# Turning the attention probabilities by a product with a diagonal tile of gate over sum

## The reference, cut to what matters

```python
pc = masked_softmax(lc, ...)          # compressed: 31 key blocks
ps = masked_softmax(ls, ...)          # selected: with 512 tokens all 8 blocks are taken, so plain causal attention
pw = masked_softmax(lw, ...)          # window of 512: causal attention again, other keys and values
o = gt[..., 0:1] * oc + gt[..., 1:2] * osel + gt[..., 2:3] * ow
```

## Time and profile before

| | us |
|---|---|
| runs, median (lowest to highest) | 2557.04 (2553.45 to 2559.98) |
| the profiled execution, its own time | 2555.5 |
| its span in the profile | 2553.8 |
| TensorE matmul busy | 2346.4 (92% of the span) |
| VectorE / ScalarE / GpSimd busy | 1055.2 / 582.3 / 1050.9 |
| mean granted TensorE clock | 0.959 of full speed |

### The profile page before, as it was taken

How to read it: one execution, slowest core, us unless ns; L and a number is a source line. 1 busy time by engine, 2 the same in 40 slices (tenths; PEclk the granted TensorE clock), 3 DMA queues, 4 the chain that set the end, 5 groups by cost and what they waited for, 6 DMA issues and landing times. The chain is left out here.

```text
span 2553.8 us, 38390 instructions
## 1 busy us (share of the span) xinstructions
PE 2346.4 (92%) x15304; PEld 1761.1 (69%) x15304; DVE 1055.2 (41%) x1959; ACT 582.3 (23%) x1339; POOL 1050.9 (41%) x920
## 2 busy tenths in 40 slices
PE   6999899789999999999996999999998999999998
PEld 4776444446777777666774768777775767777776
DVE  2001677354440232267887535354444034312421
ACT  1001566331000000135553423242331010000001
POOL 1331344245654464365653122121115546544643
PEclk9999799899999999999998999999999999999998
DMA  6632100361112211321116020020202122112211
GB/s 243 216 101 90 33 1 1 133 216 65 71 50 99 83 66 54 116 76 66 66 67 58 6 78 25 21 84 14 92 6 103 66 83 83 61 72 83 83 66 38
DMA packets 49947, 193.74 MB, mean 76 GB/s; under 512 B 15650, under 2 KB 24610, under 8 KB 33522
## 3 DMA queue, kind: packets, MB, share of 16 engines
q1 hardware_dynamic: 45490, 174.88, 20.3%
q0 software_dynamic: 3856, 15.61, 1.9%
q10 hardware_dynamic: 432, 0.88, 0.1%
HBM read 170.80 MB, written 28.81 MB: 78 GB/s over the span
## 5 line engine op out<-in xcount | busy, mean ns | idle before, releaser
L1631 PE MATMUL ps<-hid,ring 128*128 128x288 f32 x768 | 194.8, 410 | 23.0 <-DVE hid L1738 23.0
L1631 PE MATMUL ps<-xn,ring 128*128 128x288 f32 x768 | 202.7, 413 | 8.3 <-DVE xn L1722 7.8
L1631 PEld LDWEIGHTS ps<-hid,ring 128*128 128x128 f32 x768 | 146.4, 191 | 64.8 <-DVE hid L1738 24.9
L1631 PEld LDWEIGHTS ps<-xn,ring 128*128 128x128 f32 x768 | 146.6, 192 | 53.5 <-issue 8.0
L1659 ACT ACTIVATE p<-ps 128x288 f32<-128x288 f32 x48 | 19.7, 410 | 626.0 <-PE ps L1631 626.0
L218 PE MATMUL ps<-xn,ring 128*128 128x288 f32 x640 | 157.2, 409 | 3.8 <-ACTq L562 3.8
L1704 POOL TENSOR_TENSOR prod<-prod,rstd 128x1152 f32<-128x1152 f32 x32 | 83.8, 2620 | 179.7 <-DVE prod L1784 163.3
L218 PEld LDWEIGHTS ps<-xn,ring 128*128 128x128 f32 x640 | 122.6, 192 | 38.0 <-ACTq L562 3.9
L2868 PE MATMUL ps<-xn,ring 128*128 128x288 f32 x512 | 138.3, 416 | 3.6 <-PE ps L2933 3.6
L744 POOL TENSOR_SCALAR ring<-ring,fac 128x128 f32<-128x128 f32 (+2 forms) x96 | 92.2, 976 | 108.2 <-DVE fac L976 108.2
L1631 PE MATMUL ps<-x_sum,wsum 128*128 128x288 f32 x512 | 133.7, 415 | 3.2 <-DVE x_sum L1725 2.5
(11 more groups left out here) (471 smaller groups left out, 4838.1 us busy)
## 6 DMA issues: line engine op xcount, KB each, us to landing
ring<-in_w_mlp SPq DMA_DIRECT2D x64, 1024.0 KB, 4.9
ring<-in_w_gdn_in SPq DMA_DIRECT2D x16, 1024.0 KB, 4.9
ring<-in_w_nsa_in SPq DMA_DIRECT2D x10, 1024.0 KB, 8.5
ring<-in_w_gdn_z SPq DMA_DIRECT2D x8, 1024.0 KB, 4.9
x<-in_seq_state SPq DMA_DIRECT2D x4, 2048.0 KB, 8.3
out_seq_state<-x SPq DMA_DIRECT2D x4, 2048.0 KB, 11.1
ring<-in_w_gdn_out SPq DMA_DIRECT2D x8, 1024.0 KB, 5.7
out_win_old<-in_win_rows POOLq DMA_DIRECT2D x1, 8064.0 KB, 47.3
```

Of the source, the lines that this page charges most:

```text
L1631: mm = nc.tensor.matmul(S.ps[:, base + BANK[p], 0:HT], stationary(p, blk.units[pair // 4], pair % 4), moving(blk.kind, p, pair), start=pai ...
```

## The change

The probabilities are no longer scaled. GpSimd instead builds for each job and half, from the identity and `fac`, four diagonal tiles of 128 by 128 in one instruction (`diag`, two buffers), and `turn` multiplies each block of unscaled exponentials by the diagonal tile of its query tile i: the block is the stationary operand as before, the diagonal tile the moving one. The result is the block turned and each query column scaled by fac. The six GpSimd scalings and the two VectorE scalings of a job go; a transpose becomes a float32 product. `diag_set` takes the place of `scaled` and `last_scaled`, and GpSimd waits for the last turning of two jobs back before it writes `diag`. The whole diff:

```diff
--- before.py
+++ after.py
@@ -666,6 +666,7 @@
         rsum = sb("rsum", [128, 2, 2, PT])
         rcp = sb("rcp", [128, 2, PT])
         fac = sb("fac", [128, 2, 2, PT])
+        diag = sb("diag", [128, 2, 2, PT, 128])
         cneg = sb("cneg", [128, PT * NC])
         csc = sb("csc", [128, PT, 2, 40])
         cprob = sb("cprob", [128, PT, 2, NC])
@@ -674,8 +675,7 @@
         sem = S.sem
         vt_mm, vt_out, consts, neg_set = sem("pa_vt_mm"), sem("pa_vt_out"), sem("pa_consts"), sem("pa_neg_set")
         score, biased, maxed, exped = sem("pa_score"), sem("pa_biased"), sem("pa_maxed"), sem("pa_exped")
-        fac_step, fac_set, scaled = sem("pa_fac_step"), sem("pa_fac_set"), sem("pa_scaled")
-        last_scaled = sem("pa_last_scaled")
+        fac_step, fac_set, diag_set = sem("pa_fac_step"), sem("pa_fac_set"), sem("pa_diag_set")
         turned, turned_out, pv = sem("pa_turned"), sem("pa_turned_out"), sem("pa_pv")
         cmp_read, cstep, cexp, cready = sem("pa_cmp_read"), sem("pa_cstep"), sem("pa_cexp"), sem("pa_cready")
         cpv, o_done, o_out = sem("pa_cpv"), sem("pa_o_done"), sem("pa_o_out")
@@ -738,10 +738,12 @@
             nc.gpsimd.memset(csc[:], 0.0).then_inc(consts, 1)
             for job in range(NJ):
                 pool.wait_ge(fac_set, job + 1)
+                if job >= 2:
+                    pool.wait_ge(turned, chunk_no[job - 2, 1, 2] + 1)
                 for half in range(2):
-                    for i in range(PT - 1):
-                        p = prob[job % 3][half][:, p_at(i):p_at(i) + width(i)]
-                        nc.gpsimd.tensor_scalar(p, p, fac[:, job % 2, half, i:i + 1], None, ALU.mult).then_inc(scaled, 1)
+                    nc.gpsimd.tensor_tensor(diag[:, job % 2, half], S.c("ident").unsqueeze(1).broadcast_to([128, PT, 128]),
+                                            fac[:, job % 2, half].unsqueeze(2).broadcast_to([128, PT, 128]), ALU.mult
+                                            ).then_inc(diag_set, 1)
 
         @block.tensor
         def _(pe):
@@ -785,13 +787,13 @@
             def turn(job, g):
                 for half in range(2):
                     n = chunk_no[job, half, g]
-                    pe.wait_ge(scaled, (job * 2 + half + 1) * (PT - 1))
-                    pe.wait_ge(last_scaled, job * 2 + half + 1)
+                    pe.wait_ge(diag_set, job * 2 + half + 1)
                     if n >= 2:
                         pe.wait_ge(turned_out, n - 1)
                     for x, (j, i) in enumerate(blocks_of(g)):
-                        mm = nc.tensor.transpose(S.ps[:, TB + n % 2, 128 * x:128 * x + 128],
-                                                 prob[job % 3][half][:, p_at(i) + 128 * j:][:, 0:128], S.c("ident"))
+                        mm = nc.tensor.matmul(S.ps[:, TB + n % 2, 128 * x:128 * x + 128],
+                                              prob[job % 3][half][:, p_at(i) + 128 * j:][:, 0:128],
+                                              diag[:, job % 2, half, i], start=True, stop=True)
                     mm.then_inc(turned, 1)
 
             def cmp_turn(m):
@@ -971,14 +973,11 @@
                 v.reciprocal(rcp[:], rsum[:, job % 2]).then_inc(fac_step, 1)
                 dve.wait_ge(fac_step, f0 + 1)
                 if job >= 2:
-                    dve.wait_ge(scaled, (job - 1) * 2 * (PT - 1))
+                    dve.wait_ge(diag_set, (job - 1) * 2)
                 g = S.gates[:, 0:PT, :].rearrange("p i (h b) -> p h i b", b=3)[:, h0:h0 + 5:4, :, 1 + br]
                 v.tensor_tensor(fac[:, job % 2], rcp[:], g, ALU.mult).then_inc(fac_set, 1)
                 dve.wait_ge(fac_set, job + 1)
                 dve.sem_inc(fac_step, 1)
-                for half in range(2):
-                    p = prob[job % 3][half][:, p_at(PT - 1):p_at(PT - 1) + width(PT - 1)]
-                    v.tensor_scalar(p, p, fac[:, job % 2, half, PT - 1:PT], None, ALU.mult).then_inc(last_scaled, 1)
 
             def out_copy(m):
                 dve.wait_ge(pv, 2 * m + 2)
```

## The result

The changed kernel takes 2570.45 us, the median of 5 runs (2568.2 to 2574.49), against 2557.04 for the kernel before (2552.99 to 2559.98; the 2553.45 in the table above is the second lowest): a ratio of 1.0058, 95% interval [1.0042, 1.0074], 13.4 us slower. Run again later beside other kernels, on a chip where the kernel before took 2554.13, it took 2571.41: 1.0066 [1.0050, 1.0083], 17.3 us. The profiled execution is the slowest of the first five, 2574.49 us with a span of 2572.9.

A forecast was written before the change was run, and what follows sets the result against it. TensorE, busy 92% of the span, was taken as all but the bound. Steady pairs 9, opening 2.1, tail 4.7 and clock 2.5 us gave +18 on 2555.5, 2573.5; with the median 1.5 higher, 2575, range 2565 to 2589.

The forecast's parts named there:

- (a): GpSimd: six scalings, 5.76 us a job, give way to two diagonal builds, 2.1 us a job; counted as nothing.
- (b): VectorE: two scalings, 1.01 us a job, go; second unit's bias and third group's copy come earlier; no separate gain counted.
- (c): TensorE's turning: 320 more records at 0.117 us, 37.4 us more work at full clock, 2.34 us a job.
- rival E: TensorE's turning: a product here costs twice as much, 0.23 us a record; +90 us, 2647; chance 0.03.
- (d): TensorE's waits absorb part of the new records; steady pairs add 9 us, opening 2.1, tail 4.7: 15.8 at full clock.
- (e): TensorE's clock: half-speed stretches cost the full 1.7 us once waits are used up; one or two left, 2.5 us.
- the opening: Stretch before the steady pairs, 285.01 to 309.89 us, two jobs: 4.7 us more work less 2.6 absorbed, 2.1 us added.
- A: TensorE's clock stays full, small sections no longer end in a fall: +14 us, 2571; chance 0.17.
- B: TensorE's clock falls once in every pair and in the tail, all paid: +27.7 us, 2585; chance 0.17.
- C: The chain through VectorE sets the pace, so 1.01 us a step comes off: -14 us, 2543; chance 0.04.
- D: On TensorE the product costs as one record or idle time takes it all: 0 to -3 us, 2555; chance 0.09.
- signs of being wrong: Steady pair below 24.3 us; TensorE waiting for diag; clock falls in all pairs or none; a difference behind the stage.

The follow-up runs named there:

- diag_built_but_transposed: Changed kernel with the transpose by the identity put back; diag built but unused, factor gate over sum left out of two branches: 2550.0 against 2551.12 us, 0.9999.
- first_group_twice: Kernel before with only the first group's transposes, 8 of a job's 20, issued twice: 2552.25 against 2554.13 us, 0.9992.
- transposed_twice: Kernel before with every transpose of the turning issued twice into the same place: 2569.44 against 2551.12 us, 1.0074.
- gpsimd_scales_all: Kernel before with the widest row's scaling moved from VectorE to GpSimd: 2554.07 against 2551.12 us, 1.0010.
- product_by_identity: Kernel before with the turning as a float32 product with the identity, scalings kept: 2570.84 against 2551.12 us, 1.0078.
- first_copy_early: Kernel before with ScalarE's first copy of turned blocks put ahead of the step's first exponential: 2552.21 against 2554.13 us, 0.9981.

## Why the prediction was right, and where a size was off

The forecast was 18 us slower, 2575; measured were 13.4 us, 2570.45, inside the range, and 17.3 us on the second chip. The mechanism held: one more record per block, partly hidden by waits, and nothing back from the other engines. That the sum came this close is in part luck, since its errors had both signs.

(a) GpSimd, counted at nothing: right. 32 instructions of 1039 ns against the 1038 of the earlier trace rows, and no wait of a TensorE matmul on diag appears in the steady pairs.

(b) VectorE: the 1.01 us a job was said to bring the third group's copy forward. It did, in diag_built_but_transposed, but the pair stays at 23.40 us, because two other waits took the place of that one. It cost nothing in the sum, since TensorE's own growth fills these waits. What (b) missed is the step before the first turning, where the removed scaling gives back 0.5 us once.

(c) TensorE: right. 640 records, 0.119 us apart against 0.117 taken. The Trainium skill's factor of 4 between a transpose and a float32 product ("TensorE: Matmul & The Clock Gate", section "Terms") does not hold here: one product costs what two transposes cost (24.78 and 25.00 us a pair), so the factor is 2, and rival E falls.

(d) What the waits absorb: right in kind, a bit small in size. Of the 4.68 us of new records in a pair, 2.49 were to be absorbed in the walk (25.6 us) and 2.8 with the allowance (25.3 us). Measured at full clock: 25.00 - 23.41 = 1.59 us are left, so 3.1 are absorbed. Over six pairs the sum thus had 1.8 us too much. Step (e) had 2.3 us too little for them, and by luck the two errors nearly cancel: six pairs of 25.3 and 2.5 for the clock are 154.3 us, and 154.84 were measured. The tail is 4.8 us longer, where 4.7 stood.

Off was the opening: 2.1 us were added, and it came out 0.7 us shorter, because the granted clock was back at 2.4 GHz at 282 us instead of 294. Products can't be the cause, since the first turning began only at 283.93. In the ten profiles of this study the clock was back at 281 to 283 us in seven and at 291 to 294 in three. All three are of kernels with transposes in which VectorE scales; the five without that scaling are all early, and so are two with it. Whether the removed scaling, which stands ahead of this point, has a hand in it stays open. At a clock that is full throughout, the opening takes 22.61 us in first_group_twice, whose added records cost a steady pair nothing, and 24.22 in the changed kernel: 1.6 us more, as in a steady pair.

(e) The clock: right that the pattern would break, short on the count. A half-speed stretch of 3.4 us costs a pair

- 0.5 us with 320 transposes (23.93 against 23.41 in the kernel before),
- 1.4 us with the first group doubled (24.84 against 23.41),
- 1.6 us in the changed kernel (26.64 and 26.58 in its two profiles, against 25.00).

That is the claim of step (e), that waits hide it until they are used up, shown in three sizes. The count: three of six steady pairs and one in the tail, in both profiles of the changed kernel, where one or two were expected. In the steady pairs the three cost 154.84 - 6 x 25.00 = 4.8 us, against the 2.5 taken. Across the profiles, the four kernels with 320 transposes fell in four to six of the six steady pairs, the six profiles with more records in two or three. What makes the clock fall in one pair and not in the next was not settled; between 640 transposes and 640 records of products there was no difference (two and two).

Rivals: A and B both fall, since the clock neither stayed full nor fell in every pair; rival A's cause, that transposes don't count as activity, finds no support in transposed_twice. C falls by gpsimd_scales_all, D by product_by_identity, E by both.

Of the signs of being wrong one came up: a difference behind the stage, 5.9 us in the first profile of the changed kernel and 2.5 in the second, where 2 were allowed. Its cause is open.

## What to carry to other kernels

Work that an engine does in the shadow of another is worth nothing until that other engine is shown to wait for it, and the name beside a wait is to be checked against when that instruction ended: here 92 us of GpSimd scaling and 16 us of VectorE scaling were removed for no gain in the steady pairs, while one more record per block on the engine nearest to its bound cost 13 to 20 us. Before a load is put on an engine, add up its waits in one period of the loop and ask which of them stand right behind the new work: records put ahead of a wait that was long enough were free to the hundredth of a microsecond, and in the tail, where no wait could take them, they were paid in full. And taking work off a path that is not the longest can remove a wait and shorten nothing, because the next wait takes its place.

## What the runs showed of the hardware that was not expected

A float32 transpose on TensorE costs half of a float32 product of the same size (0.113 to 0.117 against two records of 0.119 us), not less. The same 3.4 us at half clock are worth 0.5 or 1.6 us to the same loop, depending on how much TensorE waits in it. And a half-speed stretch can take back what an edit gained: the 0.49 us a pair that first_copy_early gains at full clock are gone in a pair with such a stretch.
